# Two attention layers behind a recurrent one: first latent head reordered, middle modulation moved, first differential query rotated first

## The reference

```python
for i in range(2):
    shift, scale, gate = adaln(c, ada_w[i], ada_b[i])          # silu(c) @ w + b, in three parts
    h = x * (1.0 + scale) + shift                              # the same for the context
    o, o_c = mla_mixer(h, h_c, ...) if i == 0 else diff_mixer(h, h_c, ...)
    x = layer_norm(ALPHA * x + gate * (o @ out_w[i]), ln_g[i], ln_b[i])
    if i == 0:
        ctx = layer_norm(ALPHA * ctx + gate_c * (o_c @ out_w[i]), ln_g[i], ln_b[i])
```

```python
q, k, v, gate = split(h @ w_in, 4)
q, k = apply_rope(q, cos, sin), apply_rope(k, cos, sin)
o1 = softmax(q[..., 0] @ k[..., 0].T * scale) @ v
o2 = softmax(q[..., 1] @ k[..., 1].T * scale) @ v
o = rms_norm(o1 - lam_full * o2, g_sub) * (1 - lambda_init) * silu(gate)
```

## Time and profile before

| | before |
|---|---|
| executions, us | 1662.83, 1664.92, 1671.53 |
| the profiled execution's own time, us | 1661.99 |
| its span, us | 1660.2 |
| mean granted TensorE clock | 0.985 of 2.4 GHz |
| busy, us: TensorE / VectorE / ScalarE / POOL | 1575.9 / 1002.5 / 696.4 / 914.7 |
| latent start (row products of head 0 to first maximum product of head 2) | 848.50 to 873.43 |
| norm between the layers, TensorE | 1186.15 to 1208.26 |
| first differential score product | 1243.31 |

### The profile page before, as it was taken

How to read it: one execution, slowest core, us unless ns; L and a number is a source line. 1 busy time by engine, 2 the same in 40 slices (tenths; PEclk the granted TensorE clock), 3 DMA queues, 4 the chain that set the end, 5 groups by cost and what they waited for, 6 DMA issues and landing times.

```text
span 1660.2 us, 27073 instructions
## 1 busy us (share of the span) xinstructions
PE 1575.9 (95%) x10984; PEld 1277.6 (77%) x10984; DVE 1002.5 (60%) x1308; ACT 696.4 (42%) x1210; POOL 914.7 (55%) x722
## 2 busy tenths in 40 slices
PE   6999887999999999999989999999889999999887
PEld 5677887678888888878867777768778888888775
DVE  5699886747565530042556666664766666566665
ACT  4653775333222210042335555561254334444662
POOL 5354787929999989955650321345533444443152
PEclk9999999999999999999999999999999999999998
DMA  5221104422222242231120000003321110111211
GB/s 195 77 87 66 54 4 156 153 102 90 87 101 101 101 176 103 101 140 51 51 76 1 26 0 26 1 23 132 135 80 51 52 41 36 51 52 51 103 51 51
DMA packets 18875, 126.06 MB, mean 76 GB/s; under 512 B 2096, under 2 KB 2352, under 8 KB 4304
## 3 DMA queue, kind: packets, MB, share of 16 engines
q1 hardware_dynamic: 18624, 124.02, 20.5%
q10 hardware_dynamic: 144, 0.52, 0.1%
HBM read 122.43 MB, written 2.10 MB: 75 GB/s over the span
## 4 chain that ended last, share of the span: by engine, by line
PE 55%; issue 18%; POOL 12%; DVE 9%; ACT 4%; DMA 1%; POOLq 0%; ACTq 0%; SPq 0%; DVEq 0%
POOL w_hi L682 8%; PE banks L1331 5%; PE banks L1310 4%; PE banks L1488 4%; POOL w_lo L673 4%; PE banks L1491 4%; PE banks L1489 4%; PE banks L1193 3%; PE banks L1198 3%; PE banks L1194 3%; PE banks L1543 2%; PE banks L789 2%; PE banks L790 2%; PE banks L791 2%; PE banks L1523 2%
## 5 line engine op out<-in xcount | busy, mean ns | idle before, releaser
L682 POOL TENSOR_TENSOR w_hi<-raw,der 128x512 fp32r<-128x512 f32 x296 | 333.7, 1138 | 419.5 <-PE banks L1491 186.1
L673 POOL TENSOR_TENSOR w_lo<-raw,w_hi 128x512 fp32r<-128x512 f32 x336 | 479.8, 1441 | 61.9 <-ACT w_hi L1632 61.5
L789 PE MATMUL banks<-h_hi,w_hi 128*128 128x512 f32 x464 | 184.2, 397 | 0.3 <-DVEq L2316 0.3
L790 PE MATMUL banks<-h_lo,w_hi 128*128 128x512 f32 x464 | 180.7, 389 | 0.0
L791 PE MATMUL banks<-h_hi,w_lo 128*128 128x512 f32 x464 | 180.5, 389 | 0.0
L1488 PE MATMUL banks<-h_hi,w_hi 128*128 128x512 f32 (+1 forms) x384 | 146.6, 382 | 1.0 <-DVE h_lo L2901 0.8
L1489 PE MATMUL banks<-h_lo,w_hi 128*128 128x512 f32 (+1 forms) x384 | 131.2, 357 | 0.0
L2153 ACT ACTIVATE dP<-banks,der 128x768 f32<-128x768 f32 x64 | 57.8, 902 | 160.4 <-DVE der L2989 160.4
L735 POOL TENSOR_TENSOR Of<-Of,Ls 128x768 f32<-128x768 f32 x8 | 14.7, 1831 | 186.7 <-DVE Ls L2791 186.7
L1491 PE MATMUL banks<-h_hi,w_lo 128*128 128x512 f32 (+1 forms) x384 | 116.2, 357 | 0.0
L789 PEld LDWEIGHTS banks<-h_hi,w_hi 128*128 128x128 f32 x464 | 87.1, 188 | 25.9 <-issue 7.5
(11 more groups left out here) (514 smaller groups left out, 3840.3 us busy)
## 6 DMA issues: line engine op xcount, KB each, us to landing
raw<-in_stream SPq DMA_DIRECT2D x84, 1024.0 KB, 4.8
ada_home<-in_ada_w SPq DMA_DIRECT2D x18, 1024.0 KB, 6.9
raw<-in_ada_w SPq DMA_DIRECT2D x4, 1024.0 KB, 4.8
xT<-in_x_t SPq DMA_DIRECT2D x2, 1024.0 KB, 7.0
xT<-in_x_t SPq DMA_DIRECT2D x1, 2048.0 KB, 7.6
ada_end<-in_ada_w SPq DMA_DIRECT2D x2, 1024.0 KB, 5.9
out_t<-z SPq DMA_DIRECT2D x8, 256.0 KB, 2.1
ctxT<-in_ctx_t SPq DMA_DIRECT2D x1, 1024.0 KB, 6.6
```

What stands on the lines that cost most here:

```text
L673: return pool.tensor_tensor(lo[:, h, part(i), :], raw_tiles(half)[:, part(i), :], hi[:, h, part(i), :], ALU.subtract)
L682: pool.tensor_tensor(hi[:, h, part(i), :], raw_tiles(half)[:, part(i), :], one, ALU.mult).then_inc(hi_done, 1)
L789: pe.matmul(banks[b][:, :], hi, tile(rhs_hi, k), start=(at_k == 0), stop=False)
L790: pe.matmul(banks[b][:, :], hi, tile(rhs_lo, k), start=False, stop=False)
```

## The change

Three edits, one at each of the places above; the arithmetic is the same but for the order of one sum.

1. Latent start. The fill of key and value set 1 and the copy of its rotated low key part go from VectorE to POOL, behind POOL's split before the heads, each step waiting for the one before. ScalarE copies the row of head 0 ahead of the query of head 1, and the rotated high key part only behind the second exponential. TensorE makes the query of head 2 ahead of head 0's scores.
2. Middle norm. TensorE does adaLN product 7 first of all, and VectorE its columns and gains ahead of the centring. The last square is no longer added by VectorE; TensorE sums it from its own tile by a further `token_sums`. The weights of product 9 have another home (0 to 16 KB, where the residual input was), and their two DMAs wait on the last gated tile instead of product 7.
3. Differential start. The rotation comes one chunk earlier. VectorE completes the query before it turns to the key, whose product with the cosine now reads PSUM; ScalarE copies the query's high parts as soon as they are there, then the gate, then the key's. The later heads signal the query by itself, too.

```diff
@@ homes @@
-    ADA_KB = ((16, 24), (16, 24), (117, 125), (92, 109), (32, 40), (49, 136), (40, 106), (49, 57), (40, 106))
+    ADA_KB = ((16, 24), (16, 24), (117, 125), (92, 109), (32, 40), (49, 136), (40, 106), (49, 57), (0, 8))
@@ SP @@
-        ada_block(18, 14)
-        ada_block(19, 15)
+        sp.wait_ge(z_centred, KT)
+        for b in (18, 19):
+            sp.wait_ge(ada_full[b % 4], 16 * (b // 4))
+            ada_block(b)
         weights(STREAM["diff"] + 2, STREAM["diff_out"])
@@ POOL @@
+        def step(ins):
+            n = next(steps)
+            ins.then_inc(fill_step.sem, 1)
+            pool.wait_ge(*fill_step.at(n))
+
+        pool.wait_ge(split_full, before)
+        pool.wait_ge(block_done, BLK_LAST + 1)
+        for e in range(2):
+            c = slice(96, 128) if e == 0 else slice(0, 32)
+            step(pool.memset(KHI[1][e][c, :].bitcast(F32), 0.0))
+            step(pool.memset(KHI[1][e][top_at(e):top_at(e) + 1, :].bitcast(F32), 1.0))
+            step(pool.memset(KLO[1][e][c, :].bitcast(F32), 0.0))
+            step(pool.memset(VV[1][e][:, :, 64 - 64 * e:128 - 64 * e], 1.0))
+        pool.sem_inc(mla_filled.sem, 1)
+        for e in range(2):
+            r = rope_rows(e)
+            step(pool.tensor_copy(KLO[1][e][r, :], KLO[0][e][r, :]))
+        pool.sem_inc(kpe_low.sem, 1)
@@ TensorE @@
         row(0)
+        for k in range(2):
+            query(2, k)
         scores(0, 0)
...
-                    if j in (0, 2):
+                    if h and j in (0, 2):
                         query(after, j // 2)
...
         def middle_norm():
             pe.wait_ge(wide_free[0], N_MLA_USES)
+            ada_product(7)
...
-            pe.wait_ge(*x_sq_added.at(KT - 1))
-            token_sums(6, zqacc, True, True, 6).then_inc(z_sum, 1)
-            ada_product(7)
+            pe.wait_ge(*x_sq_added.at(KT - 2))
+            token_sums(6, zqacc, True, False, 6)
+            pe.wait_ge(z_sq, KT)
+            token_sums(6, zusq[:, 1, :], False, True, 6).then_inc(z_sum, 1)
...
-            if c == 19:
+            if c == 18:
                 diff_rotate(0)
@@ ScalarE @@
         mla_gate(11)
+        row_copy(0)
         query_hi(1)
-        for e in range(2):
-            ins = act.activation(KHI[1][e][rope_rows(e), :], KHI[0][e][rope_rows(e), :], ACT.Copy)
-        ins.then_inc(kpe_high.sem, 1)
-        row_copy(0)
...
             if h:
                 output_c(h - 1)
+            else:
+                for e in range(2):
+                    ins = act.activation(KHI[1][e][rope_rows(e), :], KHI[0][e][rope_rows(e), :], ACT.Copy)
+                ins.then_inc(kpe_high.sem, 1)
...
         take_q(0)
         take_k(0)
+        high_query(0)
+        take_gate(0)
         high_own(0)
         high_other(0)
-        take_gate(0)
@@ VectorE @@
         dve.wait_ge(block_done, BLK_LAST + 1)
-        fill(1)
         query_lo(1)
-        for e in range(2):
-            r = rope_rows(e)
-            ins = dve.tensor_copy(KLO[1][e][r, :], KLO[0][e][r, :])
-        ins.then_inc(kpe_low.sem, 1)
...
         x_add_tile(7, 5)
-        x_add_square(7)
+        ada_columns(7)
+        gains(0)
...
         for k in range(5, KT):
             x_centre(k)
-        ada_columns(7)
-        gains(0)
...
+        def rope_first():
+            dve.wait_ge(*rot_full.at(1))
+            dve.tensor_tensor(dtq[:, :], pairs[X_PAIR][:, 0, :], rope[:, 1, :], ALU.mult)
+            dve.tensor_tensor(dtk[:, :], pairs[X_PAIR][:, 1, :], rope[:, 1, :], ALU.mult).then_inc(rot_read.sem, 1)
+            chain.link(dve.tensor_tensor(dq[:, :], dq[:, :], rope[:, 0, :], ALU.mult))
+            dve.wait_ge(*rot_read.at(1))
+            dve.tensor_tensor(dq[:, :], dq[:, :], dtq[:, :], ALU.add).then_inc(roped.sem, 1)
+            chain.link(dve.tensor_tensor(dk[:, 0:T], wide(key_pair(0), T), rope[:, 0, :], ALU.mult))
+            dve.tensor_tensor(dk[:, 0:T], dk[:, 0:T], dtk[:, :], ALU.add).then_inc(roped.sem, 1)
```

43 lines of the change are left out of this document (23 added, 20 removed).

## The result

| kernel | median, us | lowest to highest | runs | ratio to the kernel before (95% interval) |
|---|---|---|---|---|
| before, same chip | 1662.67 | 1660.28 to 1671.53 | 6 | 1 |
| changed | 1654.72 | 1652.22 to 1656.48 | 6 | 0.9946 (0.9932 to 0.9960) |

What follows compares the result with a forecast made beforehand. TensorE, busy 95% of the span, was taken as the bound. Terms -6.5 + 0.3 - 4.4 = -10.6 us gave 1651.4 from the profiled execution or 1654.3 from the median; midway 1652.9 us, range 1648 to 1657.

Steps and rivals of the forecast that it cites:

- Part 1: Start of the latent attention: idle time, a later wait and half clock go, 6.5 us faster; 4.8 if the clock falls.
- the wait for the exponential: Latent start: with the row copy early, the exponential is late next before the first value product; 0.2 us charged.
- Part 2: Norm between the layers: 0.3 us slower in sum, bounds 1.2 faster to 2.0 slower.
- If the clock is held by product 7: Norm: column sums advance by 1.45 instead of 2.90 us, and VectorE's normalising starts about 1.2 us earlier.
- The wait for the DMA gains nothing: Norm: the 3.25 us wait before product 9 goes without gain, since a ScalarE and VectorE chain sets the end.
- The gap grows to 4.3: First differential projection: TensorE arrives earlier and its gap before the fifth tile grows from 0.8 to some 4.3 us.
- 0.50 for 3.4 us: 1.7 lost ... That costs 0.75: Behind the gap before the fifth tile: half clock loses 1.7 us, three following tiles return about 0.95, net 0.75.
- Part 3: First differential head: the 2.69 us wait before the score product and the half clock behind it go, 4.4 us faster.
- The clock's 1.7: First differential head: without the wait the clock does not fall to half, saving 1.7 us.
- Rival 1: Latent start: POOL's fill is late, TensorE stands 5.5 us and loses 1.7 to the clock; 1660.1 us, chance 0.13.
- rival 3: Latent start: POOL's fill is far dearer, 14 us late at 3 us a memset; run slower, 1668 us, chance 0.04.
- Rival 2: Attention starts and norm: gaps close but the clock falls anyway; 5.5 us gained, 1658.0 us, chance 0.15.

Runs made afterwards that it cites:

- part one alone: The kernel before with only the latent-start edits (second fill on POOL, head 2's query first, row copy first): 1657.78 us, ratio 0.9947.
- Part three alone: The kernel before with only the differential-start edits (rotation one chunk earlier, query completed before key): 1662.18 us, ratio 0.9979.

## Why the prediction was right, and where its sum was off

**Part 1: predicted 6.5, measured 6.1.** The row of head 0 to the output end went from 337.6 (four profiles) to 331.4 or 331.5 (nine that have this part and its own fill). The order of ScalarE, the two query halves at full pace, and the clock at 1.00 came as predicted, so the mechanism stands. Of the 0.4, the wait for the exponential (0.34, not 0.2) is 0.1; the rest is not traced. The fill was priced right from a memset of 120 elements: 0.74 against 0.73. By the time, part one alone is 8.8 us (5.3 to 12.2), which holds the 6.1 of the rows.

**Part 2: predicted 0.3 slower, measured nothing that the time resolves.** Its claims one by one. "If the clock is held by product 7" it is, but not for long: the column sums take 1.56 us and the first two token sums 1.40 and 1.48 in all eight profiles of the new norm, where the old one has slow token sums in three of five. The third token sum took 1.48 to 1.54 in five of the seven profiles that have it and 2.33 and 2.53 in the other two, and behind the wait for the root the clock is 0.50 in all eight. That wait, 2.1 to 2.5 us, and the half clock behind it are terms that the prediction put at nothing; on the way to the first normalising they are 0.5 us at most. The two slow third sums put it 0.5 and 0.7 us later (14.43 and 14.62 against 13.96). The Trainium skill's rule for the clock ("TensorE: Matmul & The Clock Gate", section "Part 1: The HAM clock gate"), which I weighed and did not count on, was the better guide for the sums behind product 7. By it the step would give 1.2; the normalising starts 14.1 us behind the output end in the mean of four against 14.9 in five, 0.8, and 0.2 in the first pair of profiles. "The wait for the DMA gains nothing" holds too: normalised to rotation is 25.9 to 26.3 us with the old norm, whether TensorE starts the projection 19.3 or 25.7 us behind the output end. "The gap grows to 4.3" holds: 4.0.

The term that was mis-sized is the next one, "0.50 for 3.4 us: 1.7 lost ... That costs 0.75". The rows it rests on are three, and each lasts about 3 us; in the changed kernel's profile the half clock lasted 6.4 us and took 3.2, of which the tiles' pace gave 1.3 back. Against the 25.9 of most others, normalised to rotation is 1.8 us longer in two profiles, 1.4 in a third, and 0.6 in the fourth, whose clock over that length was 0.73. So the sum of 0.3 came out near by luck: in the means the earlier normalising gives more than 0.45, and the clock takes more than 0.75 in three profiles of four. And my row for the old norm was one draw of something that moves by 2.9 us between profiles; the first comparison of two profiles, 1.7 slower, was mostly that.

**Part 3: predicted 4.4, measured 3.5.** Part three alone gives 0.9979, 3.5 us (1.5 to 5.5). The wait of 2.7 us is gone in every profile with the part, and the rows give 2.9 for it: 2.18 from the rotation to the score product (16.44 to 14.26), and 0.70 ahead of the rotation, for the piece that stands behind it now. The clock's 1.7 is the term that was mis-sized: from the first score product to the start of TensorE's last instruction it took 404.8 us in the mean of four profiles with the wait (403.9 to 405.6) and 404.0 in ten without it (403.0 to 404.6). That is 0.7, and the two ranges overlap. In the first pair of profiles the half clock did cost 1.7 by the second score product, but 0.6 of it came back within the first head and 0.7 is left at the end (405.1 against 404.4).

**Sum.** -6.1 + 0.5 (the two means of part 2) - 3.5 = -9.1, measured 9.0 us. That these agree to 0.1 is luck, since the ratio's interval is 6.6 to 11.3 us. The predicted sum of -10.6 is 1.5 us more, as parts 1 and 3 were each priced a little high and part 2 a little low; the mechanisms of parts 1 and 3 are in the rows. Rival 1 did not come, as the fill was 3.1 us early, nor rival 3. Rival 2 did not come at the attention starts: 1.00 in both. In the norm the clock did fall, behind the two new waits. Rival 3's price, written as 1658 + 10, does not follow from its terms, which give 1668.6 (14 late and 1.7 for the clock, less the 10.6); nothing hangs on it.

## What to carry to other kernels

A gap of TensorE is worth its length plus what the clock takes behind it, but that second part differs between executions of one program; read it from several profiles before a term of a sum rests on it. An engine that arrives earlier gains nothing until the chain that ends later is shortened too: here the earlier transfer and the earlier reading of columns each showed no gain, and together 4 to 5 us in the rows. Fill jobs moved to an engine with idle time are cheap as long as their end has a known reserve; compare that end with the first reader's start and not with the engine's load.

## What the runs showed of the hardware that I had not expected

- The same wait of 3.08 us left TensorE at a granted clock of 0.53 in one profile and of 1.00 in another of the same code; behind a wait of 4.0 us the half clock lasted 6.4 us in two profiles, against 2.8 to 3.5 in the rows of before.
- Behind a wait of 2.1 us for the root, with full-speed token sums ahead of it, the clock was 0.50 in one profile (the columns of product 7 back), and behind 2.3 to 2.5 us in five more. In the two others the clock had fallen already in the token sums.
- VectorE's operations on 128x8 elements with two SBUF inputs took 0.78 to 1.19 us beside POOL's split, 0.17 us with POOL idle.
- The addition of a square, 128x768 with two SBUF inputs, took 2.02 us beside the split, where an earlier one of the same line with POOL idle took 0.96 (1167.12 in the profile of before).
